# Feed forward's and gate's norms: the residual times the norm's weight is split chunk by chunk, and the root is multiplied into the products

## What is computed

```
x = x + merged @ w_out
h2 = rmsnorm(x, g_mlp)
x = x + square(relu(h2 @ w_ff1)) @ w_ff2              # 1024 -> 4096 -> 1024
ple_gate = sigmoid(rmsnorm(x, g_ple) @ w_ple_gate)
x = x + (p @ w_ple) * ple_gate
```

## Time and profile before

| | |
|---|---|
| median of 3 runs | 3810.3 us (3804.82, 3810.3, 3817.7) |
| profiled execution, its time | 3809.31 us |
| its span | 3807.5 us |
| PE busy | 3524.9 us (93%), 18417 matmuls |
| DVE, ACT, POOL busy | 2190.0, 1529.1, 734.2 us (58%, 40%, 19%) |
| mean granted PE clock | 0.971 |
| chain that ended last | PE 81%, DVE 9%, ACT 4%, DMA 3%, issue 2%, POOL 1% |

### The profile page before, as it was taken

One profiled execution on the slowest core, in us unless ns is written; L12 is line 12 of the kernel. 1 busy time (PEld: TensorE's weight loads), 2 busy tenths in 40 slices (PEclk: granted clock), 3 DMA queues, 4 the chain that ended last, 5 costly groups with the idle time before them and its releaser, 6 DMA issues.

```text
span 3807.5 us, 45943 instructions
## 1 busy us (share of the span) xinstructions
PE 3524.9 (93%) x18417; PEld 2895.9 (76%) x18417; DVE 2190.0 (58%) x2898; ACT 1529.1 (40%) x1900; POOL 734.2 (19%) x334
## 2 busy tenths in 40 slices
PE   6999999999899899999998789999769699999996
PEld 4566677677687688888886567777547699999996
DVE  3343446545366555545325444545654899999996
ACT  3344442334222221121124433333342677777774
POOL 2111111122123222222223111111011222222210
PEclk9999999999999999999999999999889899999998
DMA  3111113143553144444311113132532899999996
GB/s 126 40 50 56 56 61 123 56 149 125 188 189 127 45 138 142 151 150 149 97 39 49 58 68 135 63 117 92 155 114 80 335 378 378 380 384 382 377 378 244
DMA packets 127268, 611.68 MB, mean 161 GB/s; under 512 B 14353, under 2 KB 15769, under 8 KB 102226
## 3 DMA queue, kind: packets, MB, share of 16 engines
q1 hardware_dynamic: 122306, 591.44, 42.4%
q0 software_dynamic: 4608, 16.78, 1.7%
q10 hardware_dynamic: 144, 0.52, 0.0%
HBM read 525.39 MB, written 83.27 MB: 160 GB/s over the span
## 4 chain that ended last, share of the span: by engine, by line
PE 81%; DVE 9%; ACT 4%; DMA 3%; issue 2%; POOL 1%; SPq 0%; DVEq 0%; ACTq 0%; POOLq 0%
PE bank L264 17%; PE bank L266 17%; PE bank L265 17%; PE bank L3085 4%; PE bank L3087 4%; PE bank L3086 4%; PE bank L3097 2%; PE bank L3095 2%; PE bank L3096 2%; PE bank L616 2%; PE bank L585 1%; PE bank L594 1%; PE bank L605 1%; DVE stg L1619 1%; DVE res L854 1%
## 5 line engine op out<-in xcount | busy, mean ns | idle before, releaser
L264 PE MATMUL bank<-XH,WH 128*128 128x512 f32 (+1 forms) x2696 | 1085.2, 403 | 97.1 <-DVE XL L2018 16.2
L266 PE MATMUL bank<-XH,WL 128*128 128x512 f32 (+1 forms) x2696 | 1055.4, 391 | 0.0
L265 PE MATMUL bank<-XL,WH 128*128 128x512 f32 (+1 forms) x2696 | 1053.5, 391 | 0.0
L252 POOL TENSOR_TENSOR WL<-WR,WH 128x1024 fp32r<-128x1024 f32 (+1 forms) x249 | 494.3, 1985 | 2161.1 <-ACT WH L244 2161.1
L264 PEld LDWEIGHTS bank<-XH,WH 128*128 128x128 f32 x2696 | 512.1, 190 | 267.0 <-issue 76.8
L265 PEld LDWEIGHTS bank<-XL,WH 128*128 128x128 f32 x2696 | 513.5, 190 | 108.8 <-issue 6.3
L266 PEld LDWEIGHTS bank<-XH,WL 128*128 128x128 f32 x2696 | 512.9, 190 | 105.7
L244 ACT ACTIVATE WH<-WR 128x1024 fp32r<-128x1024 f32 (+1 forms) x249 | 216.5, 870 | 612.6 <-PE bank L266 592.0
L3026 DVE TENSOR_TENSOR EL<-ER,EH 128x2816 fp32r<-128x2816 f32 x120 | 369.1, 3082 | 4.0 <-POOL warm L3269 4.0
L3021 ACT ACTIVATE EH<-ER 128x2816 fp32r<-128x2816 f32 x120 | 306.5, 2563 | 151.7 <-PE bank L3087 89.0
L3085 PE MATMUL bank<-EH,WH 128*128 128x352 f32 x1024 | 335.6, 328 | 1.5 <-DVE WL L3187 1.5
(11 more groups left out here) (511 smaller groups left out, 5009.0 us busy)
## 6 DMA issues: line engine op xcount, KB each, us to landing
ER<-in_wu_dram SPq DMA_DIRECT2D x48, 1408.0 KB, 9.1
ER<-in_wd_dram SPq DMA_DIRECT2D x40, 1408.0 KB, 9.6
aq<-in_w_ada_dram SPq DMA_DIRECT2D x96, 512.0 KB, 3.9
WR<-in_w_in_dram SPq DMA_DIRECT2D x89, 512.0 KB, 4.5
ER<-in_wg_dram SPq DMA_DIRECT2D x32, 1408.0 KB, 8.1
res<-in_wg_dram SPq DMA_DIRECT2D x16, 1408.0 KB, 8.5
res<-in_wu_dram SPq DMA_DIRECT2D x16, 1408.0 KB, 8.6
WR<-in_wg_dram SPq DMA_DIRECT2D x16, 1408.0 KB, 8.3
```

What stands on the lines that cost most here:

```text
L252: e.tensor_tensor(WL[:, n % 2 * 1024:n % 2 * 1024 + m], raw, hi.bitcast(F32), ALU.subtract).then_inc(*w_lo.up("w_lo", n))
L264: e.matmul(bank[bk][:, 0:b - a], whi, xhi, start=k == 0, stop=False)
L265: e.matmul(bank[bk][:, 0:b - a], whi, xlo, start=False, stop=False)
L266: mm = e.matmul(bank[bk][:, 0:b - a], wlo, xhi, start=False, stop=k == K - 1)
```

## The change

- The residual's chunks get their own operands: `YH`, `YL` (where `FH`, `FL` lay). As soon as a half chunk of the residual is final, ACT writes `YH` as the residual times the norm's weight (`next_hi`, with `scale=`) and DVE writes `YL` as residual times weight less `YH` (`next_lo`). This stands in the last loop of the `w_out` stage and in the last pass of feed forward. `norm_act`, `norm_dve` and `norm_pool` are gone.
- The first half tile of feed forward and of the gate stands ahead of the sum products (`norm_pe`) on PE. The root goes to `rN`, the upper half of `stg`.
- The eviction of a `w_ff1` product is DVE's, maximum with 0 times the root, into one of two slots (`f_slot`) where there were four; ACT squares in place and copies at once. Its parts go to `XH`, `XL`.
- The gate's product goes from its bank through a multiplication with the root on DVE, and then through Tanh on ACT.
- The `w_out` stage loads x in half chunks into `ac2`, behind the residual of the half chunk before, where two full buffers of `yr` served.
- `PH`, `PL`, `pT` and a new `zs` for the gate's squares lie where `XH` lies. SP no longer waits for `ff.lo`.

```diff
-    FH, FL = sb("FH", 8 * T, F32R, c2), sb("FL", 8 * T, F32R, c2)
+    YH, YL = sb("YH", 8 * T, F32R, c2), sb("YL", 8 * T, F32R, c2)
...
+    def f_slot(i):
+        return stg[:, i % 2 * 512:i % 2 * 512 + 512]
+
+    rN = stg[:, T:2 * T]
...
-            e.wait_ge(*(on("wo.ev", m - 2, 1) if m >= 2 else on("br.ylo", 12 + m)))
-            e.dma_start(tj(yr, m % 2), I["xT"][m]).then_inc(*d_xin[m % 2].up("wo.x", m))
+            for h in range(2):
+                if m:
+                    e.wait_ge(*on("wo.ev", m - 1, h))
+                e.dma_start(ac2[:, half(h)], I["xT"][m][:, half(h)]).then_inc(*d_xin[h].up("wo.x", m, h))
...
+        e.wait_ge(*on("wo.lo", 1, 7))
         for m in range(8):
             w_split_hi(e, N_OUT + m + 2)
             for h in range(2):
+                next_hi(e, br_act, "wo", "ff", "g_mlp", m, h)
                 sum_sq_act(e, br_act, "wo", m, h)
+
+    def next_hi(e, A, key, nxt, gain, m, h):
+
+        o = m * T + h * 512
+        e.wait_ge(*on(key + ".res", m, h))
+        e.activation(YH[:, o:o + 512], xc(m)[:, half(h)], AF.Copy, scale=pr(gain, m)).then_inc(*A.up(nxt + ".hi", h, m))
+
+    def next_lo(e, V, nxt, gain, m, h):
+        o = m * T + h * 512
+        e.wait_ge(*on(nxt + ".hi", h, m))
+        e.scalar_tensor_tensor(YL[:, o:o + 512], xc(m)[:, half(h)], pr(gain, m), YH[:, o:o + 512].bitcast(F32),
+                               ALU.mult, ALU.subtract).then_inc(*V.up(nxt + ".lo", h, m))
...
-                e.wait_ge(*on("wo.x", m))
-                e.scalar_tensor_tensor(xc(m)[:, half(h)], bank[(2 * m + h) % 8][:, :], 0.5, tj(yr, m % 2)[:, half(h)],
+                e.wait_ge(*on("wo.x", m, h))
+                e.scalar_tensor_tensor(xc(m)[:, half(h)], bank[(2 * m + h) % 8][:, :], 0.5, ac2[:, half(h)],
                                        ALU.mult, ALU.add).then_inc(*V.up("wo.ev", m, h))
                 on.at["wo.res", m, h] = on.at["wo.ev", m, h]
                 sum_sq_dve(e, V, "wo", m, h)
+                if m + h == 0:
+                    e.wait_ge(*on("wo.lo", 1, 7))
+                next_lo(e, V, "ff", "g_mlp", m, h)
...
-    def norm_act(e, A, key):
...
-    def norm_dve(e, V, key, gain):
...
-    def norm_pool(e, G, key):
...
     def ff_pe_(e):
-        norm_pe(e, NORM_FF)
...
-            x = xs(T, FH, FL, f % 2 * 4 * T) if two else xs(T)
+            x = xs(T, XH, XL, f % 2 * 4 * T) if two else xs(T, YH, YL)
...
+                if t + h == 0:
+                    norm_pe(e, NORM_FF)
...
-        norm_act(e, A, NORM_FF)
+        rstd_act(e, rN, 1024, T, (6, 7), ("ff",))
...
-            e.activation(FH[:, o:o + 512], q_slot(i), AF.Copy).then_inc(*A.up("ff.fhi", i))
+            e.activation(XH[:, o:o + 512], f_slot(i), AF.Copy).then_inc(*A.up("ff.fhi", i))
...
-                    e.wait_ge(*on("gemm", N_FF + t, h * 512))
-                    if i >= 4:
-                        e.wait_ge(*on("ff.flo", i - 4))
-                    e.activation(q_slot(i), bank[(2 * t + h) % 4][:, :], AF.Relu).then_inc(*A.up("ff.ev", t, h))
-                    on.at["ff.relu", i] = A.now
-                    if i % 8:
-                        hi(i - 1)
-                    if i % 8 == 7:
-                        hi(i)
+                    e.wait_ge(*on("ff.ev", t, h))
+                    e.activation(f_slot(i), f_slot(i), AF.Square).then_inc(*A.up("ff.sq", i))
+                    hi(i)
                 elif f == 7:
+                    next_hi(e, A, "ff", "ple", "g_ple", m, h)
...
-                e.wait_ge(*on("ff.lo", 1, 6))
+                e.wait_ge(*on("ff", "sum", 1))
...
-                    q = q_slot(i)
-                    e.wait_ge(*on("ff.relu", i))
-                    e.tensor_tensor(q, q, q, ALU.mult).then_inc(*V.up("ff.sq", i))
+                    e.wait_ge(*on("gemm", N_FF + t, h * 512))
+                    e.wait_ge(*on("ff", "rstd", h))
+                    if i >= 2:
+                        e.wait_ge(*on("ff.flo", i - 2))
+                    e.scalar_tensor_tensor(f_slot(i), bank[(2 * t + h) % 4][:, :], 0.0, rN[:, half(h)], ALU.max,
+                                           ALU.mult).then_inc(*V.up("ff.ev", t, h))
...
+                        next_lo(e, V, "ple", "g_ple", m, h)
...
     def ple_pe(e):
-        norm_pe(e, NORM_PLE)
...
+                    if m + two + h == 0:
+                        norm_pe(e, NORM_PLE)
...
-                e.wait_ge(*on("gemm", N_PLE + 2 * m, h * 512))
-                if m:
-                    e.wait_ge(*on("ple.res", m - 1, h))
-                else:
-                    e.wait_ge(*on("ple.lo", 1, 4 + h))
-                    e.wait_ge(*on("ple.lo", 1, 7))
-                e.activation(q_slot(h), bank[(4 * m + h) % 8][:, :], AF.Tanh, scale=0.5).then_inc(
-                    *A.up("ple.ev", m, 0, h))
+                e.wait_ge(*on("ple.ev", m, 0, h))
+                e.activation(q_slot(h), q_slot(h), AF.Tanh, scale=0.5).then_inc(*A.up("ple.tanh", m, h))
...
+                q = q_slot(h)
+                e.wait_ge(*on("gemm", N_PLE + 2 * m, h * 512))
+                e.wait_ge(*on("ple", "rstd", h))
+                if m:
+                    e.wait_ge(*on("ple.res", m - 1, h))
+                e.tensor_tensor(q, bank[(4 * m + h) % 8][:, :], rN[:, half(h)], ALU.mult).then_inc(
+                    *V.up("ple.ev", m, 0, h))
+            for h in range(2):
                 q, rs = q_slot(h), xc(m)[:, half(h)]
-                e.wait_ge(*on("ple.ev", m, 0, h))
+                e.wait_ge(*on("ple.tanh", m, h))
```

More of the change, by code:

```diff
@@ L1400, in program @@
     c2 = ExitStack()
-    FH, FL = sb("FH", 8 * T, F32R, c2), sb("FL", 8 * T, F32R, c2)
+    YH, YL = sb("YH", 8 * T, F32R, c2), sb("YL", 8 * T, F32R, c2)
     c2.close()
+    c1.close()
     c2 = ExitStack()
     PH, PL, pT = sb("PH", 2 * T, F32R, c2), sb("PL", 2 * T, F32R, c2), sb("pT", 2 * T, c=c2)
+    zs = sb("zs", T, c=c2)
     c2.close()
-    c1.close()
     br_act, br_dve, br_pool = sem("act_branch"), sem("dve_branch"), sem("pool_branch")
@@ L1591, in norm_pe @@
         rstd_pe(e, acq, T, (6, 7), (key[1],))
-    def norm_act(e, A, key):
[L1594 to L1599, removed]
-    def norm_dve(e, V, key, gain):
[L1603 to L1614, removed]
-                if i >= 4:
[L1616 to L1622, removed]
-    def norm_pool(e, G, key):
[L1625 to L1629, removed]
-                                ALU.subtract).then_inc(*G.up(key[1] + ".lo", h, j))
     FF = []
@@ L1636, in program @@
         FF += [(f - 1, 1, m) for m in range(8)] if f else []
-    NORM_FF, NORM_PLE = ("wo", "ff", N_FF - 1), ("ff", "ple", N_PLE - 1)
+    NORM_FF, NORM_PLE = ("wo", "ff"), ("ff", "ple")
     def ada_of(t):
@@ L1644, in ff_sp @@
     def ff_sp(e):
-        for h in range(2):
-            for j in range(8):
-                e.wait_ge(*on("ff.lo", h, j))
         for i in range(2):
@@ L1716, in ff_dve_ @@
         V = ff_dve
-        norm_dve(e, V, NORM_FF, "g_mlp")
         def lo(i):
@@ L1722, in lo @@
             e.wait_ge(*on("ff.fhi", i))
-            e.tensor_tensor(FL[:, o:o + 512], q_slot(i), FH[:, o:o + 512].bitcast(F32), ALU.subtract).then_inc(
+            e.tensor_tensor(XL[:, o:o + 512], f_slot(i), XH[:, o:o + 512].bitcast(F32), ALU.subtract).then_inc(
                 *V.up("ff.flo", i))
@@ L1769, in ff_pool_ @@
     def ff_pool_(e):
-        norm_pool(e, ff_pool, NORM_FF)
         for t in range(96):
@@ L1788, in ple_pe @@
                     e.wait_ge(*on.bank(bk, "ple.ev", m, two, h))
-                    gemm(e, N_PLE + 2 * m + two, xs(T, PH, PL) if two else xs(T), h * 512, h * 512 + 512, bk, h == 1,
-                         (lambda k: e.wait_ge(*on("ple.lo", h, k))) if m == 0 and not two else None)
+                    gemm(e, N_PLE + 2 * m + two, xs(T, PH, PL) if two else xs(T, YH, YL), h * 512, h * 512 + 512, bk,
+                         h == 1, (lambda k: e.wait_ge(*on("ple.lo", h, k))) if m == 0 and not two else None)
+                    if m + two + h == 0:
+                        norm_pe(e, NORM_PLE)
     def ple_act(e):
         A = pl2_act
-        norm_act(e, A, NORM_PLE)
+        rstd_act(e, rN, 1024, T, (6, 7), ("ple",))
         join(e, "ff")
@@ L1815, in ple_act @@
                         e.wait_ge(*on("ple.add", i - 1, 0))
-                    e.activation(q_slot(2), xc(m)[:, half(h)], AF.Square).then_inc(*A.up("ple.sq", i, 0))
+                    e.activation(zs[:, half(0)], xc(m)[:, half(h)], AF.Square).then_inc(*A.up("ple.sq", i, 0))
                     if i > 2:
                         e.wait_ge(*on("ple.add", i - 1, 1))
-                    e.activation(q_slot(3), xc(m)[:, half(h)], AF.Square, scale=pr("g_final", m)).then_inc(
+                    e.activation(zs[:, half(1)], xc(m)[:, half(h)], AF.Square, scale=pr("g_final", m)).then_inc(
                         *A.up("ple.sq", i, 1))
@@ L1828, in ple_dve @@
         V = pl2_dve
-        norm_dve(e, V, NORM_PLE, "g_ple")
         for h in range(4):
@@ L1838, in add @@
```

(3 more changed lines are left out.)

## The result

The changed kernel took **3786.8 us** (median of 4 runs, 3783.8 to 3788.7) beside 3810.7 for the kernel before (4 runs, 3804.8 to 3817.7): ratio 0.9939, 95% interval 0.9926 to 0.9951, 23.9 us less. The forecast was 3778, 32 less, with a range of 3766 to 3792. The profiled execution took 3788.06 with a span of 3786.2 us, mean clock 0.971 as before.

A forecast was written before the change was run, and what follows sets the result against it. Chains of waits through two norms bound the kernel there, matmuls in plain feed forward. Terms 19.4 + 16.9 - 4.4 = 31.9 us off the profiled 3809.3 gave 3777.4, forecast as 3778 with 0.6 given back; range 3766 to 3792.

The forecast's parts named there:

- What bounds the kernel: Plain feed forward is bound by matmuls at full clock; both norms by a chain of waits, over 52.0 and 36.5 us.
- Second norm, gain 20.2: Between `w_out` and feed forward tile t=2: t=2 starts 31.8 us behind the last `w_out` matmul instead of 52.0.
- The 0.8 for the clock: Ahead of t=2: 0.8 us deducted for possible clock halving after 2.8 us idle, leaving net 19.4.
- Feed forward itself, 0: Feed forward tiles and last pass: moved evictions, later weight splits and smaller `x` loads are covered, costing 0 us.
- Rival B: Feed forward: evictions queue on VectorE behind `w_ada` reductions waiting for DMA; slower, 3819 us; chance 0.04.
- Third norm, gain 16.9: From the last feed forward matmul to the second gate tile: 19.6 us instead of 36.5.
- a time 1.4 us longer: Third norm: the skill's drain of about 1.38 us per table switch would lengthen the wait ahead of `w_ple`; not priced.
- Gate tiles 2 to 7, loss 4.4: Gate stage: VectorE's multiplication ahead of the next weight split adds 0.69 + 0.05 us, six times.
- Rival A: Gate and last feed forward pass: VectorE and POOL collide, giving back 9.1 + 4 us; 3791 us; chance 0.12.
- The range: Whole kernel time: 3766 to 3792 us, leaving out the unlikely rivals and the far ends of others.
- the forecast's own interval: Whole kernel time: 3771 to 3787 us around the forecast of 3778, chance 0.70.
- What the prediction said would show it: Signs in the trace, among them a gate tile's period of 15.9 to 16.3 us instead of 15.2 to 15.7.

## Why the prediction was right and where it was not

**What bounds the kernel: right.** The chain through both norms was the cost; with it taken apart the tensor engine is busy for 27.6 of 31.8 and 16.4 of 19.7 us, and feed forward did not move.

**Second norm, gain 20.2: right, step by step.** Sum products, diagonals and t=2 start 6.9, 14.4 and 31.75 us behind the last `w_out` matmul, for 6.9, 14.4 and 31.8. Both small idles are there, 1.42 and 2.77, and the kernels with t=2 split early and with chunk 7 first show that each had the cause named: the weight split behind the eviction of t=0, and chunk 7 behind the weight split. `YL` of chunk 7 was held under POOL's split (VectorE from 1294.86 to 1297.2, 2.38 us for 0.75) and was there 4.1 us behind `w_out`, ahead of its use at 4.8, as forecast. The 0.8 for the clock was a mean: the first profile had no halving behind the idle of 2.8 us; of the nine profiles with that idle (2.5 to 2.8) six had one, at 1.5 us.

**Feed forward itself, 0: right.** 681.3 in both first profiles. Rival B (eviction queued behind the `w_ada` reductions, 3819) has nothing for it: no idle in 681 us. The margin of 5 us in an 11 us tile held.

**Third norm, gain 16.9: right**, 36.5 to 19.6, with 0.8 idle ahead of `w_ple` for 1.1 forecast, and POOL's split 0.2 longer. The table load takes 1.28 us and the next instruction starts 0.01 us behind it, as in the earlier trace rows, so the drain that the Trainium skill (ScalarE: Activation LUTs, What ACT_TABLE_LOAD costs) adds is absent here too, and a time 1.4 us longer was rightly left out.

**Gate tiles 2 to 7, loss 4.4: this step failed; it measured 12.6.** The count and the 0.74 for each multiplication were right, 4.5 us; the kernel with VectorE's product moved isolates it as 16.15 for 15.41. Three things were not in the term:
- *The clock, 5.5 us net.* The prediction priced a halving ahead of t=2, where the idle is 2.8 us, but not at the gate tiles, where the multiplication and POOL's hold bring the idle from 1.4 to 2.5. Four of seven tiles began at 1.2 GHz: 1.61, 1.58 and 1.42 us over the 16.49 of full clock, and 1.54 at the last tile. That is 6.15. From it go 0.6, by which three steps of the kernel before are longer than 15.41; these are its tiles with the slower matmuls, and against its repeat (113.5) the loss is 13.2. A rise of idle by 1.1 us cost nearly as much in clock (6.15) as in waiting (six times 1.08).
- *POOL's hold, 2.0 us*, 0.33 in each of six steps. Rival A saw the collision from the other side only: VectorE held by POOL. That occurs (2.04 us for 0.69 in the timeline above) and costs the tensor engine nothing that shows: multiplication and POOL's 0.33 alone make up the full-clock step's 1.08 us over 15.41. What costs is POOL held by VectorE, since the split then came later than VectorE's product. The Trainium skill (SBUF — State Buffer, SBUF: two separate sides) has the rule: of a VectorE instruction with two SBUF inputs and a GpSimd one that reads SBUF, whichever starts first keeps the shared ports and the other waits. The trace agrees in direction, with 0.33 us for an overlap of 0.50; the prediction had used only the half of it that the earlier trace rows shows.
- *The end of the last tile, 0.5 us* (21.58 us at full clock for 21.08): the multiplication stands in that path too, without a next gate tile behind it.

4.5 + 2.0 + 5.5 + 0.5 = 12.5, against 12.6 measured. The forecast was 8.2 us off in this term, and the time lies 8.8 above it. Rival A's time (3791) was nearer to the result than the forecast's, by another mechanism than the one it gave: its hold on VectorE lengthened no step, and the last pass of feed forward, where it put 4 us, lost none.

**The range** held the time. That 3786.8 also lies inside the forecast's own interval (3771 to 3787) is luck, by 0.2 us: its profiled execution took 3788.1, and the later runs gave 3789.8 and 3788.4. The centre was wrong for the gate term above, and the first profile has 3.3 us more in stretches that the change does not touch, which the forecast put at nothing. What the prediction said would show it (a gate tile's period of 15.9 to 16.3) showed it: 16.49 to 18.10.

## What to carry to other kernels

When an edit lengthens an idle of the tensor engine by a microsecond, price the clock with the wait, at every place where it occurs: in the gate idles up to 1.7 us never halved it, and from 2.1 us on it was halved behind about half of them, each for some 1.5 us. When an instruction is put on a path, look at what shares that path's queue and is not needed for it: a weight split moved ahead of one Tanh paid back the whole 12.6 us and 3.9 more. And compare stretches between the same matmuls, not only total times, where the total of one kernel varies by 10 us and more for reasons outside the change.

## What the runs showed that was not expected

- **Idle and clock.** Number of gate tiles that began at 1.2 GHz, or fell to it in their first 1.5 us, by the idle ahead of them: none of 7 with the split first (one idle of 1.7 us and six of 0.9) and none with the multiplication left out (one of 0.4, six of 1.4), 3 of 7 at 2.1, 4 of 7 at 2.5 in all five profiles with it, 3 of 7 at 3.1 (2.8 to 3.7). It is a step and then a share, not a slope. Nor is the share a coin: in all five profiles at 2.5 us the second, third and fifth gate tile are halved, and the eighth or, in two of them, the seventh. And length alone does not decide: none of the three idles of 2.17 us ahead of the sum products of the old third norm was followed by half clock, and ahead of t=2 the three idles without a halving are among the longest (2.64, 2.69 and 2.77, beside 2.52 to 2.68 for the six with one). What else decides is open.
- **POOL held by VectorE.** 2.70 us for 2.37 where VectorE's product starts 0.19 us ahead of the split, gone when that product waits.
- **A slower matmul at full granted clock.** 0.2333 us for 0.2289 from start to start, 430 for 439 matmuls in 100 us without idle. In two of eleven profiles it held for the whole of feed forward from t=2 on, 13 us; in others for single gate tiles, 0.2 us each. It began behind an idle and ended where the engine next stopped. The granted clock says 1.00 throughout, so it is found only by counting matmuls or by their steps.
